# One sum of expert outputs in memory instead of two, and the last two blocks added by TensorE

## The reference, cut to what matters

```python
def routed_experts(h, top_e, top_w, w_gate, w_up, w_down):
    ...                               # rows sorted by expert, in blocks of 128
    def expert_block(args):
        tok, e = args
        xb = h_pad[tok]
        hid = jax.nn.silu(xb @ w_gate[e]) * (xb @ w_up[e])
        return hid @ w_down[e]
    yb = lax.map(expert_block, (row_tok.reshape(n_blocks, MOE_BLOCK), block_e))
    yb = yb.reshape(rows, d) * row_w[:, None].astype(yb.dtype)
    return jax.ops.segment_sum(yb, row_tok, num_segments=t + 1)[:t]

def moe_ffn(h, ...):
    top_e, top_w = route(h, w_router, router_bias)      # 6 of 64 experts for each token
    routed = routed_experts(h, top_e, top_w, w_gate, w_up, w_down)
    shared = (jax.nn.silu(h @ ws_gate) * (h @ ws_up)) @ ws_down
    return routed.astype(h.dtype) + shared
# y = layer_norm(ALPHA * h + moe_ffn(h))
```

## Time and profile before

| | |
|---|---|
| runs | 1412.91, 1414.36 and 1414.99 us; median 1414.36 |
| profiled execution | 1414.54 us, span 1412.8 us, mean granted TensorE clock 0.955 |
| busy in the span | PE 1248.9 us (88%), DVE 1112.4 (79%), ACT 867.7 (61%), POOL 742.5 (53%) |
| DMA | 335 MB, mean 237 GB/s |

### The profile page before, as it was taken

How to read it: one execution, slowest core, us unless ns; L and a number is a source line. 1 busy time by engine, 2 the same in 40 slices (tenths; PEclk the granted TensorE clock), 3 DMA queues, 4 the chain that set the end, 5 groups by cost and what they waited for, 6 DMA issues and landing times.

```text
span 1412.8 us, 23627 instructions
## 1 busy us (share of the span) xinstructions
PE 1248.9 (88%) x6341; PEld 1060.3 (75%) x6341; DVE 1112.4 (79%) x1479; ACT 867.7 (61%) x1049; POOL 742.5 (53%) x585
## 2 busy tenths in 40 slices
PE   4799989987999999599999999999999999999930
PEld 3699989974788777478888888788878778787720
DVE  6927976763789986589999989799888879798828
ACT  7522112106556542278888878788787878787736
POOL 1018647520000147238888887688767767686610
PEclk9899999998999999899999999999999999999965
DMA  9333564429243343479899999999999999999676
GB/s 273 135 91 65 93 61 63 63 32 336 87 160 120 121 148 106 155 304 315 327 361 344 374 336 348 331 345 361 328 345 320 340 326 336 339 329 336 168 215 249
DMA packets 113891, 335.05 MB, mean 237 GB/s; under 512 B 30448, under 2 KB 61168, under 8 KB 89248
## 3 DMA queue, kind: packets, MB, share of 16 engines
q1 hardware_dynamic: 88160, 280.19, 56.2%
q0 software_dynamic: 24464, 53.72, 15.7%
q10 hardware_dynamic: 1200, 0.38, 0.1%
HBM read 288.77 MB, written 70.61 MB: 254 GB/s over the span
## 4 chain that ended last, share of the span: by engine, by line
DMA 30%; PE 20%; DVE 4%; ACT 1%; issue 1%; SPq 1%; ACTq 1%; DVEq 0%; POOLq 0%
DMA rt_raw_up<-in_w_up_dram 28%; PE moe_p_gu L2303 11%; PE moe_p_dn L2315 6%; PE moe_p_tr L2327 2%; DVE moe_dn_l L2414 1%; DVE rt_raw_up L2460 1%; DVE rt_raw_up L2461 1%; ACT moe_dn_h L2154 1%; DMA rt_raw_up<-acc 1%; SPq L2029 1%; DVE rt_raw_up L2467 1%; DMA rt_raw_dn<-in_w_down_dram 1%; ACTq L2018 0%; PE moe_p_ht L2335 0%; DMA acc<-rt_raw_up,moe_idx_t 0%
## 5 line engine op out<-in xcount | busy, mean ns | idle before, releaser
L2383 DVE TENSOR_TENSOR moe_up_l<-rt_raw_up,moe_up_h 128x2048 fp32r<-128x2048 f32 x150 | 343.5, 2291 | 83.1 <-ACT moe_up_h L2100 82.8
L2100 ACT ACTIVATE moe_up_h<-rt_raw_up 128x2048 fp32r x150 | 287.5, 1918 | 44.6 <-DMA rt_raw_up<-in_w_up_dram 44.6
L2303 PE MATMUL moe_p_gu<-moe_up_h,moe_x_h 128*128 128x512 f32 x608 | 240.7, 396 | 6.5 <-DVE moe_x_l L2397 5.5
L2303 PE MATMUL moe_p_gu<-moe_up_h,moe_x_l 128*128 128x512 f32 x608 | 240.4, 395 | 0.0
L2303 PE MATMUL moe_p_gu<-moe_up_l,moe_x_h 128*128 128x512 f32 x608 | 240.3, 395 | 0.0
L2238 POOL DMA_INDIRECT moe_xg<-tok,moe_idx_g x76 | 185.3, 2438 | 60.3 <-POOL moe_idx_g L2235 38.9
L2250 POOL DMA_INDIRECT acc<-moe_y,moe_idx_s x72 | 169.8, 2358 | 61.6 <-POOL moe_idx_s L2247 55.1
L2414 DVE TENSOR_TENSOR moe_dn_l<-rt_raw_dn,moe_dn_h 128x2048 fp32r<-128x2048 f32 x74 | 168.8, 2281 | 1.4 <-ACT moe_dn_h L2154 1.4
L1390 POOL DMA_INDIRECT slots<-proj_pay,proj_dst x54 | 55.1, 1020 | 188.4 <-DVE proj_dst L1698 173.2
L2247 POOL COPY moe_idx_s<-keep_small 128x1 int32 (+1 forms) x72 | 115.0, 1597 | 53.9 <-ACT moe_y L2132 53.9
L2154 ACT ACTIVATE moe_dn_h<-rt_raw_dn 128x2048 fp32r x74 | 142.0, 1919 | 1.7 <-issue 1.7
(11 more groups left out here) (465 smaller groups left out, 2676.0 us busy)
## 6 DMA issues: line engine op xcount, KB each, us to landing
rt_raw_up<-in_w_gate_dram SPq DMA_DIRECT2D x64, 1024.0 KB, 9.4
rt_raw_up<-in_w_up_dram SPq DMA_DIRECT2D x64, 1024.0 KB, 21.5
rt_raw_dn<-in_w_down_dram SPq DMA_DIRECT2D x64, 1024.0 KB, 17.1
acc<-rt_raw_dn SPq DMA_DIRECT2D x18, 512.0 KB, 3.1
co_win<-in_w_in_dram SPq DMA_DIRECT2D x16, 512.0 KB, 5.1
rt_raw_up<-acc SPq DMA_DIRECT2D x12, 512.0 KB, 13.0
resid<-trunk_x SPq DMA_DIRECT2D x9, 512.0 KB
proj_res<-resid SPq DMA_DIRECT2D x9, 512.0 KB, 3.4
```

Source lines behind the costliest of these rows:

```text
L2100: act.activation(up_h[:, par, half, :, :], raw_up[:, bass.ds(slot, 1), half, :, :].rearrange("p a k n -> p (a k) n"), ACT.Copy).then_inc(u ...
L2303: mm = pe.matmul(p_gu[:, par, :].rearrange("p (a n) -> p a n", a=2), x, w, start=(i == 0), stop=(i == len(terms) - 1))
L2383: low = tt(up_l[:, par, half, :, :], raw_up[:, bass.ds(slot, 1), half, :, :].rearrange("p a k n -> p (a k) n"), up_h[:, par, half, :, :].b ...
```

## The change

There is one sum `acc` in memory. In the routing stage the scaled copy of the tile and its store go; instead SP loads each tile of `tok` back (`reload`), DVE makes ALPHA times it plus the shared expert's result from PSUM (`with_residual`), and SP stores that. In the expert stage all scatters add into `acc`, and each waits for the landing of the one before. The last two blocks aren't scattered: ACT and DVE split their results into `dn_h` and `dn_l` in SBUF, POOL and DVE make one-hot matrices from their token numbers (`token_ids`, `is_equal`), PE multiplies those for every tile (`pick_rows`), and DVE adds the product from PSUM to the loaded tile of `acc`.

```diff
# routing stage, SP
-                sp.dma_start(io.acc[0][j * P:(j + 1) * P, :], ax[:, q % 2, :]).then_inc(s_acc[q % 2], 16)
+                sp.dma_start(io.acc[j * P:(j + 1) * P, :], ax[:, j % 2, :]).then_inc(s_acc[j % 2], 16)
+
+            def reload(j):
+                sp.wait_ge(s_tok[j % 2], 16 * (j // 2 + 1))
+                if j >= 2:
+                    sp.wait_ge(s_acc[j % 2], 16 * (j // 2))
+                sp.dma_start(ax[:, j % 2, :], io.tok[j * P:(j + 1) * P, :]).then_inc(s_ax[j % 2], 16)
...
-                sp.wait_ge(s_ax, i + 1)
-                sp.dma_start(io.acc[1][i * P:(i + 1) * P, :], ax[:, i % 2, :]).then_inc(s_acc[i % 2], 16)
...
             finished(LAST)
+            reload(0)
+            reload(1)
             store(0)
             prefetch(1)
             for j in range(1, LAST):
                 store(j)
+                reload(j + 1)
# routing stage, ACT: scaled(i) and shared(j) go, with their calls and waits
-                act.mul(ax[:, i % 2, :], x[:, i % 2, :], ALPHA).then_inc(s_ax, 1)
-                act.activation(ax[:, q % 2, :].rearrange("p (h n) -> p h n", h=2), po[:, 1, :, :], ACT.Copy).then_inc(s_out, 1)
# routing stage, DVE
+            def with_residual(j):
+                v.wait_ge(s_pd, j + 1)
+                v.wait_ge(s_ax[j % 2], 16 * (j // 2 + 1))
+                rows = ax[:, j % 2, :].rearrange("p (h n) -> p h n", h=2)
+                stt(out=rows, in0=rows, scalar=ALPHA, in1=po[:, 1, :, :], op0=ALU.mult, op1=ALU.add).then_inc(s_out, 1)
...
             in_low(LAST + 4)
+            with_residual(0)
             choose_groups(LAST)
             place(LAST - 5)
             hidden(2)
...                                   # likewise 1 to 4, behind in_low of each turn
             hidden(6)
             order_experts()
 
             hid_low(6)
             in_low(LAST + 9)
+            with_residual(5)
             hidden(7)
             block_rows()
 
             hid_low(7)
+            with_residual(6)
             block_counts()
             write_tables()
...
             hidden(LAST)
 
+            with_residual(7)
             hid_low(LAST)
+            with_residual(LAST)
# expert stage, SP
-            wait(sp, added[0], dma_count(second, 0))
+            wait(sp, added[1], dma_count(third, 1))
             sp.sem_inc(sp_go, 1)
-            EARLY = 3
...
             for i in range(N_TILES):
-                sp.dma_start(total[i], io.acc[1][i * P:(i + 1) * P, :]).then_inc(s_x[i], 16)
-                if EARLY <= i + EARLY - 1 < N_TILES:
-                    load_first(i + EARLY - 1)
+                sp.dma_start(total[i], io.acc[i * P:(i + 1) * P, :]).then_inc(s_x[i], 16)
# expert stage, ACT
-            y_tail_out(second, 0, p_tr[:, :, :])
-            y_tail_out(last, 1, p_dn[:, :, :])
+            def y_high(n, k, src):
+                wait(act, down_done, n + 1)
+                act.activation(dn_h[:, k, :].rearrange("p (h n) -> p h n", h=2), src[:, :, :], ACT.Copy).then_inc(dn_h_done, 1)
+            y_high(second, 0, p_tr)
+            y_high(last, 1, p_dn)
# expert stage, POOL
                 wait(pool, index_s, n + 1)
                 pool.sem_inc(go, 1)
-                pool.indirect_dma_start(out=io.acc[par], in_=y[:, par, :], in_offset=None,
+                if known(n, 1):
+                    wait(pool, added[1 - par], dma_count(n - 1, 1 - par))
+                    pool.sem_inc(go, 1)
+                pool.indirect_dma_start(out=io.acc, in_=y[:, par, :], in_offset=None,
...
+            def token_ids(last):
+                pool.tensor_copy(idx_f[:, :], idx_t[:, 2:4]).then_inc(s_ids, 1)
+                wait(pool, up_l_done, last + 1)
+                pool.sem_inc(go, 1)
+                pool.iota(ids_i, pattern=[[1, N_TILES * P]], base=0, channel_multiplier=0).then_inc(s_ids, 1)
+                pool.wait_ge(s_ids, 2)
+                pool.tensor_copy(ids, ids_i).then_inc(s_ids, 1)
...
-            scatter_tail(fourth, 0, 0, y[:, 0, :])
-            scatter_tail(third, 1, 1, y[:, 1, :])
-            scatter_tail(second, 0, 2, y_tail[0])
-            scatter_tail(last, 1, 3, y_tail[1])
+            token_ids(last)
+            scatter_tail(fourth, 0, 0)
+            scatter_tail(third, 1, 1)
# expert stage, PE
+            def pick_rows(i, k):
+                for h in range(2):
+                    for m2, part in enumerate((dn_h, dn_l)):
+                        mm = pe.matmul(sums_of[i % 3][:, h, :], pick[k][:, i, :], part[:, k, 512 * h:512 * (h + 1)],
+                                       start=(k + m2 == 0), stop=(k + m2 == 2))
+                return mm
+            pe.wait_ge(s_pick, 2)
+            wait(pe, dn_l_done, second + 1)
+            pick_rows(0, 0)
+            pick_rows(1, 0)
+            wait(pe, dn_l_done, last + 1)
+            for i in range(N_TILES):
+                if i >= 3:
+                    pe.wait_ge(s_sum, i - 2)
+                if i >= 2:
+                    pick_rows(i, 0)
+                pick_rows(i, 1).then_inc(s_ps, 1)
# expert stage, DVE
             tail_low(last, 1)
+            v.wait_ge(s_ids, 3)
+            for k in range(2):
+                v.tensor_scalar(pick[k], ids.rearrange("p (i t) -> p i t", t=P), idx_f[:, k:k + 1], None,
+                                ALU.is_equal).then_inc(s_pick, 1)
             hid_tail_low(last, 1)
+            def y_low(n, k, src):
+                wait(v, dn_h_done, n + 1)
+                tt(dn_l[:, k, :].rearrange("p (h n) -> p h n", h=2), src[:, :, :],
+                   dn_h[:, k, :].rearrange("p (h n) -> p h n", h=2).bitcast(F32), ALU.subtract).then_inc(dn_l_done, 1)
+            y_low(second, 0, p_tr)
+            y_low(last, 1, p_dn)
...
-                    v.wait_ge(s_x[i], 32)
-                    tt(total[i], total[i], first_acc[i], ALU.add).then_inc(s_sum, 1)
+                    v.wait_ge(s_x[i], 16)
+                    v.wait_ge(s_ps, i + 1)
+                    rows_i = total[i].rearrange("p (h n) -> p h n", h=2)
+                    tt(rows_i, rows_i, sums_of[i % 3][:, :, :], ALU.add).then_inc(s_sum, 1)
```

More of the change, by code:

```diff
@@ L1331, in _ @@
                 in_high(i + 1)
-                if i:
-                    scaled(i - 1)
-                else:
+                if i == 0:
                     row_scales(0)
@@ L1886, in _ @@
             in_low(LAST + 5)
+            with_residual(1)
             choose_experts(LAST)
@@ L1892, in _ @@
             in_low(LAST + 6)
+            with_residual(2)
             place(LAST - 3)
@@ L1898, in _ @@
             in_low(LAST + 7)
+            with_residual(3)
             place(LAST - 1)
@@ L1903, in _ @@
             in_low(LAST + 8)
+            with_residual(4)
             place(LAST)
@@ L1971, in expert_stage @@
         lng, lnb = piece(12), piece(13)
-        y_tail = [first_acc[N_TILES - 1], total[N_TILES - 1]]
+        ids = raw_up[:, 2, 1, :, :].rearrange("p k n -> p (k n)")[:, 0:N_TILES * P]
+        ids_i = raw_up[:, 3, 1, :, :].rearrange("p k n -> p (k n)")[:, 0:N_TILES * P].bitcast(I32)
+        pick = [x[:, :, :, :].rearrange("p a k t -> p (a k) t")[:, KD // 2:KD // 2 + N_TILES, :] for x in (x_h, x_l)]
+        sums_of = [p_gu, p_tr, p_dn]
         def tail_split(w, k):
@@ L2067, in _ @@
             early = sp.value_load(rt.tab[0:1, ENDS, N_EXP:N_EXP + 1], min_val=N_EXP - BEFORE, max_val=P - 8 - BEFORE)
-            second, last = early + (BEFORE - 2), early + (BEFORE - 1)
-            sp.wait_ge(tail_l_done, 2)
+            last, third = early + (BEFORE - 1), early + (BEFORE - 3)
             wait(sp, up_l_done, last + 1)
@@ L2073, in _ @@
             sp.dma_start(lnb, io.ln2_b[0].partition_broadcast(P)).then_inc(s_lnb, 16)
-            wait(sp, added[0], dma_count(second, 0))
-            sp.sem_inc(sp_go, 1)
-            EARLY = 3
-            def load_first(i):
-                sp.dma_start(first_acc[i], io.acc[0][i * P:(i + 1) * P, :]).then_inc(s_x[i], 16)
-            for i in range(EARLY):
-                load_first(i)
-            wait(sp, added[1], dma_count(last, 1))
+            wait(sp, added[1], dma_count(third, 1))
             sp.sem_inc(sp_go, 1)
             for i in range(N_TILES):
-                sp.dma_start(total[i], io.acc[1][i * P:(i + 1) * P, :]).then_inc(s_x[i], 16)
-                if EARLY <= i + EARLY - 1 < N_TILES:
-                    load_first(i + EARLY - 1)
+                sp.dma_start(total[i], io.acc[i * P:(i + 1) * P, :]).then_inc(s_x[i], 16)
             for i in range(N_TILES):
@@ L2210, in _ @@
             act.activation(warm[:, :], eps[:, :], ACT.Sqrt)
-            wait(act, up_l_done, last + 1)
-            act.sem_inc(act_go, 1)
-            y_tail_out(second, 0, p_tr[:, :, :])
-            y_tail_out(last, 1, p_dn[:, :, :])
+            y_high(second, 0, p_tr)
+            y_high(last, 1, p_dn)
             for i in range(N_TILES):
@@ L2244, in scatter @@
                     for k in range(2):
```

(19 more changed lines are left out.)

35 lines of the change are left out of this document (10 added, 25 removed).

## The result

The changed kernel took 1477.6 us (median of four runs, 1475.7 to 1480.6) against 1413.8 us before: ratio 1.0447, interval 1.0431 to 1.0464, slower by 4.5%. The prediction was 1491. The profiled execution's span is 1475.7 us, 62.9 more than before. Times are compared between executions with the usual granted clock; one of run 4's two executions (2121 us at a mean clock of 0.56) is left out.

A forecast was written before the change was run, and what follows sets the result against it. The prediction took the block loop, with DMA engines and PE both near full, as the main bound; 1414.5 + 82 (loop) + 5 (routing stage) - 10 (end) = 1491 us, range 1420 to 1540.

The forecast's parts named there:

- The loop: Block loop: each scatter waits for the landing before; interval rises from 9.84 to 11.0 us over 71 intervals, +82 us.
- restart: Block loop: time from a scatter's landing to the next scatter's start, put at 0.77 us.
- the two fixed points: Block loop: landings of 6.3 us in quiet and 11.5 us at today's load of 0.98; 10.2 taken between them.
- Rival 1: Block loop: landings below 9.1 us hide the wait, leaving only +5 - 10, so 1409 us; chance 0.14.
- estimate of 3.2 us: Block loop: scatter landing by the page's rule, 2.0 us fixed plus bytes over 436 GB/s; would hide the wait, 1409 us.
- Rivals 2: Block loop: partial relief, intervals of 9.9 to 10.2 us, +4 to +25, so 1414 to 1435 us; chance 0.07.
- 3: Block loop: no relief, intervals over 11.7 us, from 1541 up to 1582 us; chance 0.06.
- POOL's idle time: Block loop: POOL idles before each scatter until the previous scatter's DMA ends, 1 to 2 us each.
- The end: After the loop: two serial scatters and nine of 18 loads go, so DVE's first normalisation comes earlier, -10 us.
- The routing stage: Before the loop: nine residual passes on DVE, 1.35 us each and partly hidden, add +5 us; ends 0 and +9.
- The two early periods: Routing stage: two early periods take on about 1.2 us each from DVE's residual passes, +2.4 us.
- the step that named `with_residual(5)` behind `order_experts`: Routing stage: this pass stands behind `order_experts`, and PE's down(6) waits behind it, +1.35 us.

The follow-up runs named there:

- run 4: Changed kernel loading a quarter of each expert's gate and up weights and half of the down weights: 1384.9 us (one run).
- Run 1: Kernel before, still with two sums, plus only the wait of each scatter for the landing of the one before: 1479.6 us, ratio 1.0453.
- run 3: Changed kernel loading only half of each expert's gate and up weights: 1393.5 us, ratio 0.9866 to the kernel before.
- run 2: Changed kernel without the wait for the scatter before; odd blocks' scatters add into a second array nobody reads: 1409.3 us, ratio 0.9975.
- run 5: Kernel before with two sums and the one-hot end alone; POOL adds the two sums, DVE the one-hot rows: 1420.4 us, ratio 1.0058.
- run 12: As run 2, with DVE's whole residual pass of tile 5 moved ahead of `order_experts`: ratio 0.996 to the kernel before.
- run 7: Changed kernel with each scatter split into two of 512 columns, each waiting only for the same half before: 1562.6 us, ratio 1.1038.
- Run 6: As run 2, with each of DVE's nine residual additions cut from 1024 to 128 columns: 1405.7 us, ratio 0.9947 to the kernel before.
- run 10: As run 8, with the one-hot products of three tiles issued ahead of the wait for a load: 1408.4 us, ratio 0.9958.
- run 8: As run 5, but PE brings the first sum into PSUM by identity products, with no load beside the last scatter: 1412.3 us, 0.9975.

## Why the prediction was right, step by step

**The loop** is the step that decides, and it held: a wait that no slack absorbs, T = landing + restart, a new balance between the two fixed points. Run 1 shows that it is the wait, runs 3 and 4 that the landing follows the load of the engines. The DMA share came out at 0.90 (0.87 predicted), the median landing at 10.1 (10.2), the restart near 0.8 (0.77). PE's busy share fell to 0.92 (0.87 predicted). The interval is 10.73, not 11.0, so +63 instead of +82. Of the 71 intervals 61 are what the prediction says all are, a landing and a restart: 10.86 us on average (10.05 + 0.82, rounded). The other ten are 9.92 on average. There the landing (7.48 on average) came ahead of the next start by 2.4 us on average, and the start hung on something else in POOL's list, eight times on the index copy. So the mis-sized terms are the landing, put at 10.2 instead of 10.05, worth 61 x 0.14 = 8.5 us, and the number of steps: about one interval in seven isn't of the serial chain, worth 10 x 1.08 = 11 us. The two make the 19.

Rival 1 (hidden) needed landings below 9.1 us and got 10.1; run 4 shows what it looks like where it holds. The Trainium skill's page DMA: Bandwidth & Descriptors (Anatomy of one DMA), from which the forecast took an estimate of 3.2 us for such a DMA, would have made this rival true; no loop scatter in runs 1 to 4 with a recorded landing lands in less than 5.0. Rivals 2 and 3 did not come.

POOL's idle time was foreseen at 1 to 2 us per scatter and is 4.2. POOL was busy for 330.85 of 600 us, 447.70 before: its scatter instructions have a median of 1.62 us instead of 2.85. That isn't the change, since runs 5 and 12, whose loops have no new wait, show 1.60 too; why some executions have the short ones is open.

**The end** was foreseen at -10 and is -9.9. First addition 3.4 us behind the landing of the scatter of `third` (3.5 foreseen); y_low at 1.23 and one-hot passes at 0.81 us (1.25 and 1.44). That removing the pause ahead of the first normalisation would bring it to 4.3 us behind the first addition was wrong: a wait of 1.34 us for a load is still there, 5.0. And only the last of the two removed scatters ran by itself: that of `second` started at 1355.46, while that of `third` was still under way; the gain goes by when the loads can start, which is as forecast.

**The routing stage** was foreseen at +5. From the stage's first product on PE to the token gather it takes 258.6 us on average in the five profiles that have the new stage with nothing moved or shortened (after, runs 2, 3, 4 and 7), and 252.8 in the five that have the old one: +5.8. The sum came out, but its terms did not. Ahead of the mark the new stage is about 1.1 us quicker, for a reason that no run separates. Behind the mark the token gather is 6.8 us later. The two early periods, put at +2.4, show +1.4 at DVE's last slot index (65.6 us from the mark instead of 64.2), and with_residual(5) adds its 1.3: the list gather's 2.7 to 2.8. Run 6 confirms these, since it gives them back with short passes.

Between the list gather and the token gather 1.35 was foreseen and 4.0 came (9.84 us instead of 5.83). Right was the step that named `with_residual(5)` behind `order_experts` with PE's down product behind it. It was priced at the pass; it costs PE a wait of 2.40 us and then 12 products 0.43 us apart instead of 0.23, since the granted clock fell: 12 x 0.20 = 2.4 more. That reaches ACT and, behind the list index, DVE, which waits 2.49 us for ACT and then makes with_residual(6), 1.1 more. Run 12, with the pass moved, has no such wait.

Taken apart: the wait +64 (run 1, 0.0453 x 1413, give or take 7), the rest -3.5 (run 2); together 60.5, and 63.8 was measured, within run 1's interval. That the total came within 14 us of 1491 is in part luck: the loop's 19 us too many were partly made up by scatters that started 9.9 us later, not 5, and 4.0 of that is not the change.

## What to carry to other kernels

Before two buffers are merged into one, look at how long a write takes to land beside the interval between writes. If the landing is the longer, the merge makes a serial chain whose step is a landing under that load, and what it saves elsewhere must be set against the step's excess over today's interval, times the number of steps. Here the one-hot end was worth its 10 us. About 4.3 of these can be had without the merge, as run 10 shows (from the last scatter in the loop to the end 73.9 us; 78.2 before, 68.3 with the merge): there the second sum is added by TensorE, which has time, and GpSimd, which slowed VectorE in run 5, stays idle.

## What the hardware showed that was not expected

- While GpSimd added 128x1024 tiles in SBUF, VectorE's passes that read only SBUF took 2.06 to 3.27 us instead of 1.28; its addition that reads PSUM stayed at 1.22 (run 5). With GpSimd idle the passes took 1.28 again (run 8).
- Half-size scatters (512 columns a row) land in a median of 8.0 us where whole ones take 10.1; with two of them in place of one a block took 11.89 us instead of 10.73 (run 7).
- TensorE sat idle for 1.86 us and, after 0.5 us of work, for another 2.40 us; the 12 products behind this came at the lower of its two clock levels, 0.43 us apart instead of 0.23. The granted clock between 560 and 580 us is 0.84, where the kernel before has 1.00.
- Indirect scatters that add to memory land later as the 16 DMA engines fill: medians of 7.9, 8.5, 10.1 and 11.5 us at busy shares of 0.71, 0.84, 0.90 and 0.98 between 700 and 1300 us (runs 4 and 3, the changed kernel, the kernel before).
